# A two-block network on one core: sums of the second layer in PSUM banks, squares gathered by VectorE, modulation tiles loaded as their places become free

## The reference, cut to what matters

```python
shift, scale, gate = split(silu(c) @ w_mod[l] + b_mod[l], 3)            # modulation, also for ctx
hx = rmsnorm(x, norm_g[l]) * (1 + scale) + shift                        # hc from ctx likewise
q, k, v, g_att, u_pool, g_pool, a_conv, b_conv, g_conv = split(hx @ w_in[l])
y_att  = rmsnorm(diff_attention(q, k, v), subln_g) * silu(g_att)
y_pool = (window_means(u_pool) - u_pool) @ w_pool * silu(g_pool)        # windows of 2, 4, 8, 16
u      = a_conv * sigmoid(b_conv)
y_conv = silu(layernorm(conv31(u))) @ w_pw2 * silu(g_conv)              # 31 taps, one filter per channel
x = x + gate * (concat(y_att, y_pool, y_conv) @ w_out[l])               # layer 0 updates ctx as well
```

## Time and profile before

| what | value |
|---|---|
| median of three runs | 3333.49 us |
| the profiled execution's own time | 3337.83 us |
| its span (first to last instruction) | 3336.1 us |
| mean granted TensorE clock | 0.972 of full |
| PE busy | 3139.7 us, 94% of the span |
| POOL busy | 1888.6 us, 57% |
| ACT, DVE busy | 1443.5 us, 1289.0 us |
| loads | 609 MB, 183 GB/s over the span |

### The profile page before, as it was taken

One profiled execution on the slowest core, in us unless ns is written; L12 is line 12 of the kernel. 1 busy time (PEld: TensorE's weight loads), 2 busy tenths in 40 slices (PEclk: granted clock), 3 DMA queues, 4 the chain that ended last, 5 costly groups with the idle time before them and its releaser, 6 DMA issues.

```text
span 3336.1 us, 64404 instructions
## 1 busy us (share of the span) xinstructions
PE 3139.7 (94%) x25962; PEld 2818.9 (84%) x25962; DVE 1289.0 (39%) x2057; ACT 1443.5 (43%) x2177; POOL 1888.6 (57%) x756
## 2 busy tenths in 40 slices
PE   6899999999899996999798999899989999999999
PEld 4688887777677995878787888799989999999999
DVE  2138502555101418047305787585423343332000
ACT  3212222566322431247534676565444555554333
POOL 1234543333233558445453655576866888887887
PEclk9999999999899997999898999999999999999999
DMA  9787222211443881223584676444543555554555
GB/s 367 310 334 308 88 101 75 78 68 59 186 168 126 327 328 51 101 101 115 204 350 158 249 271 236 179 152 141 187 151 140 189 177 188 179 185 164 190 189 188
DMA packets 85970, 613.35 MB, mean 184 GB/s; under 512 B 9536, under 2 KB 10816, under 8 KB 12736
## 3 DMA queue, kind: packets, MB, share of 16 engines
q1 hardware_dynamic: 84672, 606.02, 49.3%
q10 hardware_dynamic: 1152, 5.24, 0.4%
HBM read 609.13 MB, written 2.10 MB: 183 GB/s over the span
## 4 chain that ended last, share of the span: by engine, by line
issue 58%; POOL 41%; POOLq 1%; PE 0%; DVE 0%; DVEq 0%
POOL w_low L549 41%; POOLq L544 0%; POOLq L548 0%; POOLq L549 0%; PE bank L585 0%; PE bank L587 0%; PE bank L586 0%; DVE region L2343 0%; DVEq L2343 0%; POOLq L2354 0%
## 5 line engine op out<-in xcount | busy, mean ns | idle before, releaser
L549 POOL TENSOR_TENSOR w_low<-raw,w_high 128x1024 fp32r<-128x1024 f32 x752 | 1888.4, 2525 | 1441.1 <-ACT w_high L1108 1438.3
L585 PE MATMUL bank<-h_high,w_high 128*128 128x256 f32 (+1 forms) x4416 | 1412.5, 320 | 48.5 <-POOL w_low L549 47.1
L586 PE MATMUL bank<-h_low,w_high 128*128 128x256 f32 (+1 forms) x4416 | 1390.6, 315 | 0.0
L587 PE MATMUL bank<-h_high,w_low 128*128 128x256 f32 (+1 forms) x4416 | 1390.5, 315 | 0.0
L1108 ACT ACTIVATE w_high<-raw 128x1024 fp32r<-128x1024 f32 x752 | 786.5, 1054 | 1140.0 <-PE bank L587 670.2
L585 PEld LDWEIGHTS bank<-h_high,w_high 128*128 128x128 f32 x4416 | 846.5, 192 | 136.6 <-issue 44.2
L587 PEld LDWEIGHTS bank<-h_high,w_low 128*128 128x128 f32 x4416 | 845.9, 192 | 51.1
L586 PEld LDWEIGHTS bank<-h_low,w_high 128*128 128x128 f32 x4416 | 846.5, 192 | 49.9 <-issue 0.7
L1108 ACT ACTIVATE region<-bank 128x512 f32<-128x512 f32 (+3 forms) x353 | 163.8, 472 | 390.8 <-PE bank L587 308.5
L563 PE MATMUL bank<-region,vec_sb 128*32 128x128 f32 x6016 | 197.3, 283 | 40.5 <-DMA region<-in_w_mods 40.5
L563 PEld LDWEIGHTS bank<-region,vec_sb 128*32 128x32 f32 x6016 | 164.5, 113 | 74.4 <-DMA region<-in_w_mods 46.0
(11 more groups left out here) (227 smaller groups left out, 3390.7 us busy)
## 6 DMA issues: line engine op xcount, KB each, us to landing
region<-in_w_mods SPq DMA_DIRECT2D x188, 1024.0 KB, 8.0
raw<-in_w_in SPq DMA_DIRECT2D x172, 1024.0 KB, 4.9
raw<-in_w_up SPq DMA_DIRECT2D x88, 1024.0 KB, 4.8
raw<-in_w_out SPq DMA_DIRECT2D x48, 1024.0 KB, 5.4
raw<-in_w_down SPq DMA_DIRECT2D x48, 1024.0 KB, 4.9
raw<-in_w_abr SPq DMA_DIRECT2D x8, 1024.0 KB, 4.9
raw<-in_w_sbr SPq DMA_DIRECT2D x8, 1024.0 KB, 4.8
region<-in_xin SPq DMA_DIRECT2D x1, 4096.0 KB, 14.3
```

Source lines behind the costliest of these rows:

```text
L549: nc.gpsimd.tensor_tensor(WL[s][:, part], RAW[s][:, part], WH[s][:, part], ALU.subtract) \
L585: nc.tensor.matmul(bank[:, 0:n], WH[slot][:, w], h, start=first and j == 0, stop=False)
L586: nc.tensor.matmul(bank[:, 0:n], WH[slot][:, w], l, start=False, stop=False)
L587: end = nc.tensor.matmul(bank[:, 0:n], WL[slot][:, w], h, start=False, stop=last and j == len(blocks) - 1)
```

## The change

1. **Sums in banks.** In layer 1, `small` accumulates the convolution in banks `AUX[0]` and `AUX[3]` and the pooling sums in `AUX[1]` and `AUX[2]`, not in SBUF. Two copies bring the convolution back to SBUF; the final subtraction of the pooling part reads the banks and is four instructions, not one. Layer 0 stays as it is.
2. **Squares on DVE.** ACT squares as before. DVE adds each square to `AUX[0]` (`add_square`), one after the residual of the next tile; the last sum goes to `NT_` in SBUF, and one matmul with ones sums it over the partitions.
3. **Modulation tiles.** In layer 1's input product SP no longer waits for `n_hl`. After `two(1)` it waits until the output product of layer 0 has left the banks, loads the first four modulation tiles, and goes on with `two(2)`. In its output product SP issues `two(1)` (units 2 and 3) first, then two modulation tiles when four heads are gated and two more when all eight are. For that the places of `BUF_OUT1` are in another order.
4. **Distance in the queue.** The weight units keep their place relative to the turn: of the first turn, the loads that were issued already are left out.

```diff
-    BUF_OUT1 = r2(0, 2048, 4096, 6144)
+    BUF_OUT1 = r2(0, 4096, 2048, 6144)
...
-            def with_mods(turns, unit0, per, buffers, i0=0):
+            def with_mods(turns, unit0, per, buffers, after=0, asked=0, loaded=0):
                 slots = len(buffers)
-                with sp.Fori(0, turns) as i:
+                if asked:
+                    for t in range(4):
+                        for q in range(max(per * t, asked), per * (t + 1)):
+                            sp.wait_ge(sem("mod_mm"), unit0 + q - slots + 1)
+                            mod_load(buffers[q % slots], q % slots, unit0 + q)
+                        if t >= loaded:
+                            unit(0, t + 2 + after)
+                with sp.Fori(1 if asked else 0, turns) as i:
...
-                        unit(i, t + 2 + 4 * i0)
+                        unit(i, t + 2 + after)
...
                 if l == 1:
                     two(0)
                     two(1)
-                sp.wait_ge(sem("n_hl"), H_AT[f"in{l}"] + KT)
+                    evacuated(sp, T_OUT[0] + 16)
+                    for q in range(4):
+                        mod_load(BUF_IN1[q], q, M_IN1 + q)
+                else:
+                    sp.wait_ge(sem("n_hl"), H_AT["in0"] + KT)
                 two(2)
...
-                    with_mods(4, M_IN1, 2, BUF_IN1, 1)
+                    with_mods(4, M_IN1, 2, BUF_IN1, 4, 4)
...
-                sp.wait_ge(sem(f"at{l}_y"), 8)
                 if l == 0:
+                    sp.wait_ge(sem("at0_y"), 8)
                     with_mods(3, M_OUT0, 1, BUF_OUT0)
                 else:
-                    with_mods(3, M_OUT1, 2, BUF_OUT1)
+                    two(1)
+                    for q in range(4):
+                        sp.wait_ge(sem("at1_y"), 4 + 4 * (q // 2))
+                        mod_load(BUF_OUT1[q], q, M_OUT1 + q)
+                    with_mods(3, M_OUT1, 2, BUF_OUT1, 0, 4, 2)
...
-                        if end == 4 or s >= 2:
-                            add_squares(name, width, 4 * i + (s - 2), s % 2, end == 1 and s == 2, False)
-            for k in (14, 15):
-                add_squares(name, width, k, k % 2, False, k == 15)
+            pe.wait_ge(sem("n_sums"), N_AT[name])
+            nc.tensor.matmul(AUX[0][:, 0:width], ONES, NT_[:, 3, 0:width], start=True, stop=True) \
+                .then_inc(sem("n_squsd"), 1)
...
+        def add_square(name, n, i, s):
+            count = 16 * N_AT[name] + s + 1 + 4 * i
+            static = isinstance(i, int)
+            dve.wait_ge(sem("n_sq"), count)
+            sq, sums = NT_[:, s % 2, 0:n], AUX[0][:, 0:n]
+            if static and i == 0 and s == 0:
+                V.tensor_copy(sums, sq).then_inc(sem("n_squsd"), 1)
+                return
+            dve.wait_ge(sem("n_squsd"), count + 1)
+            if static and i == 3 and s == 3:
+                add(NT_[:, 3, 0:n], sums, sq).then_inc(sem("n_sums"), 1)
+            else:
+                add(sums, sums, sq).then_inc(sem("n_squsd"), 1)
...
+            in_banks = lambda n0, n1: [AUX[n][:, a:a + T] for n in (n0, n1) for a in (0, T)]
+            conv = in_banks(0, 3) if l else [y[:, 4 + c, :] for c in range(4)]
+            pools = in_banks(1, 2) if l else [y[:, g, :] for g in range(4)]
...
-                    acc = st(y[:, 4 + c, :])[:, :, a:b]
+                    acc = st(conv[c])[:, :, a:b]
...
+            if l:
+                for n in range(2):
+                    own.mark(V.tensor_copy(y[:, 4 + 2 * n:6 + 2 * n, :], AUX[3 * n][:, 0:T2].rearrange("p (c t) -> p c t", t=T)))
+                own.wait()
...
-                    acc = st(y[:, g, :])[:, :, a:b]
+                    acc = st(pools[g])[:, :, a:b]
...
-            sub(y[:, 0:4, :], y[:, 0:4, :], up).then_inc(sem("cv_pool"), 1)
+            for g in range(4):
+                last = sub(y[:, g, :], pools[g], up[:, g, :])
+            last.then_inc(sem("cv_pool"), 1)
...
+                square_before(("in1", "fin")[l], T2, i, s)
...
+            add_square(("in1", "fin")[l], T2, 3, 3)
```

More of the change, by code:

```diff
@@ L473, in stream @@
                     two(1)
-                sp.wait_ge(sem("n_hl"), H_AT[f"in{l}"] + KT)
+                    evacuated(sp, T_OUT[0] + 16)
[3 more added lines that the diff above has]
+                    sp.wait_ge(sem("n_hl"), H_AT["in0"] + KT)
                 two(2)
                 if l == 0:
-                    with_mods(3, M_IN0, 4, BUF_IN0, 1)
+                    with_mods(3, M_IN0, 4, BUF_IN0, 4)
                     start = 9
                 else:
-                    with_mods(4, M_IN1, 2, BUF_IN1, 1)
+                    with_mods(4, M_IN1, 2, BUF_IN1, 4, 4)
                     start = 11
@@ L1717, in norm, with square_before @@
                     low(at_, j, [(lo(j), T_BANK["in1"][j % 4][:, lower], unit + j, col, hi(j))])
+        def add_square(name, n, i, s):
[11 more added lines that the diff above has]
+                add(sums, sums, sq).then_inc(sem("n_squsd"), 1)
+        def square_before(name, n, i, s):
+            if s:
+                add_square(name, n, i, s - 1)
+            elif not (isinstance(i, int) and i == 0):
+                add_square(name, n, i - 1, 3)
         def rope(l, h):
@@ L1741, in small @@
             wdw, bdw = VEC["w_dw"][0] + l * 124, VEC["b_dw"][0] + 4 * l
+            in_banks = lambda n0, n1: [AUX[n][:, a:a + T] for n in (n0, n1) for a in (0, T)]
+            conv = in_banks(0, 3) if l else [y[:, 4 + c, :] for c in range(4)]
+            pools = in_banks(1, 2) if l else [y[:, g, :] for g in range(4)]
             for c in range(4):
-                own.mark(V.tensor_scalar(y[:, 4 + c, :], uc[:, c, :], VE[:, wdw + 31 * c + 15:wdw + 31 * c + 16],
+                own.mark(V.tensor_scalar(conv[c], uc[:, c, :], VE[:, wdw + 31 * c + 15:wdw + 31 * c + 16],
                                          VE[:, bdw + c:bdw + c + 1], ALU.mult, ALU.add))
@@ L1761, in small @@
             for g in range(4):
-                own.mark(V.tensor_copy(y[:, g, :], up[:, g, :]))
+                own.mark(V.tensor_copy(pools[g], up[:, g, :]))
             for off in [o_ for h in range(8) for o_ in (-1 - h, h + 1)][:15]:
@@ L1773, in small @@
                 for s in range(S):
-                    own.mark(mul(st(y[:, g, :])[:, s, :], st(y[:, g, :])[:, s, :], rc[:, g, :]))
+                    own.mark(mul(st(pools[g])[:, s, :], st(pools[g])[:, s, :], rc[:, g, :]))
             own.wait()
-            sub(y[:, 0:4, :], y[:, 0:4, :], up).then_inc(sem("cv_pool"), 1)
+            for g in range(4):
+                last = sub(y[:, g, :], pools[g], up[:, g, :])
+            last.then_inc(sem("cv_pool"), 1)
             dve.wait_ge(sem("cv_sum"), l + 1)
@@ L2308, in _, with residual2 @@
         dve.wait_ge(sem("x_norm"), KT)
-        with dve.Fori(0, 4) as i:
+        def residual2(i, s):
+            n = 4 * i + s
+            dve.wait_ge(halves_done, 2 * U_OUT2 + 2 * n + 2)
+            V.scalar_tensor_tensor(tile(RES, n), L[s][:, 0:T], MODF[:, ds(3 * n + 3 * 128 + 2, 1)], tile(RES, n),
+                                   ALU.mult, ALU.add).then_inc(bank_free[s], 1)
+            square_before("b2", T, i, s)
+        for s in range(4):
+            residual2(0, s)
+        with dve.Fori(1, 4) as i:
             for s in range(4):
[L2311 to L2314, removed]
+                residual2(i, s)
+        add_square("b2", T, 3, 3)
         evacuated(dve, T_OUT2 + 16)
```

## The result

Four runs of the changed kernel gave a median of 3256.43 us (3254.95 to 3260.75), four runs of the kernel before beside them 3330.47 us (3326.89 to 3334.86). The ratio is 0.9779, with an interval of 0.9761 to 0.9797. The forecast was 3254 us, in a range of 3243 to 3278. The profiled execution took 3255.04 us, its span is 3253.3 us.

The account below looks back on a forecast made before the run. PE, busy for 94% of the span, was taken to bound the kernel. 34.4 + 29.0 + 6.0 + 10.5 = 79.9 us off the median of 3333.49 gave 3253.6, said as 3254 us, range 3243 to 3278.

Parts of the forecast that it names:

- Part 1: Layer 1's convolution: with sums in banks POOL no longer stalls beside DVE, nor PE behind it; 34.4 us, bounds 31.7 to 37.
- The rival in which the write or the pointer operand holds POOL: Layer 1's convolution: not the second SBUF input locks POOL out, so banks change nothing; 3288 us, chance 0.08 (stall stays in part).
- The slower rival: Layer 1's sums in banks: a slow write and read-back makes DVE late for PE; above 3333 us, chance 0.03.
- Part 2: Output products of layer 0, layer 1 and second block: squares leave PE, 29.9 less 0.9 for tails, 29.0 us, bounds 26 to 31.
- so 0.6 more: Tail of layer 1's output product: one DVE addition, one matmul and semaphores take 1.8 us after a wait of 1.22 before.
- the 13 x 0.94 us of `in1`: Layer 0's output product: 13 squares ahead of the last product leave PE, 0.94 us each, 12.2 us.
- 13 x 0.42: Second block's output product: 13 squares of 256 columns leave PE, 0.42 us each, 5.5 us.
- Part 3: Layer 1's input and output products: first modulation tiles loaded earlier; 6.0 us (bounds 4.1 to 9.9) and 10.5 us (7 to 13).
- the 0.5 us that the prediction allowed: Layer 1's input product: the tiles behind the early four land at 1121, PE wants them at 1120, some 0.5 us late.
- The clock near 1.00: Sign for part 3: at the head of both layer 1 products, waits of 4.07 and 5.37 us gone, clock near 1.00.
- That the loads bind: Rival in layer 1's output product: saved squares become waits for tiles, early pairs only move waits; 3268 to 3282 us, chance 0.17.
- The estimate of 8.8 us for a tile: Layer 1's output product by the skill's 358 GB/s: squares there give 0.35 us each, not 0.94; sum 72 us.

Follow-up runs that it names:

- the undone part: The changed kernel with one part of the change taken back: without part 1 3293.46 us, without part 2 3280.52 us, without part 3 3271.3 us.
- the pair with the exchanged operands: The changed kernel, layer 1's convolution not accumulated: both tensor inputs in SBUF and output in a bank, 3295.84 us; one input in a bank and output in SBUF, 3259.37 us.

## Why the prediction was right, and where its sizes were off

**Part 1** was right in mechanism and size. The forecast of 34.4 us came from the tiles leaving the banks; the undone part gives 34.4 by the trace. The reading of the earlier trace rows, that one input in a bank leaves POOL free, was the right one, and the pair with the exchanged operands has shown it. The rival in which the write or the pointer operand holds POOL is false.

**The slower rival** is false too. The 120 instructions of the sums in banks take 46.09 us, against 46.60 in SBUF: a chain in a bank costs nothing more than one in SBUF. The rival needed 0.4 us more for each.

**Part 2** was mis-sized: 29.0 us forecast, 24.1 by the undone part. DVE's residuals show where. From the third tile's to the last's `in1` takes 171.7 us before and 161.8 after, `fin` 118.5 and 106.8; from the first's to the last's `b2` takes 91.8 and 86.5. That is 9.9 + 11.7 + 5.3 = 26.9 us for the squares ahead of the last product, where 29.9 was forecast, and the tails cost 2.6 and not 0.9. Both terms are off.

The first is "so 0.6 more ... in `in1` and `b2` ... 0.3 and 0" for the tails. They cost 9.84 - 8.29 = 1.55 us in `in1` and 10.63 - 9.88 = 0.75 in `fin`, 0 to 0.3 in `b2`. The prediction counted one addition of DVE at 0.69 and a matmul at 1.02. ACT does its last two squares one behind the other, so two additions stand in a row behind them. And the matmul of `in1` takes 2.01, behind 2.50 us in which PE has nothing to do. The squares that it used to sum there kept its clock up: with them on PE no trace shows a slow matmul in a tail, without them nine of fourteen do. So the 0.75 of `fin` is a lucky case; in three other traces it is 1.7.

The second is the 13 x 0.94 us of `in1`, which came to 9.9 us and not 12.2. Every fourth tile the square covered a wait that it had hidden: `mod_unit` has to wait until DVE has read the four sums. The timeline of PE at such a tile:

```profile
905.71 0.95 PE L587 MATMUL bank<-const_sb,region 128*128 128x4 f32 x8
907.00 1.08 PE L579 MATMUL bank<-region,vec_sb 128*32 128x128 f32 x32 [0.34 <-DVE mod_sb L1849]
```

From the sums to the next tile it takes 1.29 us now. Before it took 1.84 with the square in between, so the square's leaving gives 0.55 there, not 0.94. The other tiles are 12.13 us apart (DVE's residual begins at 919.23, 931.37 and 943.50) against 12.98 before. That fits the 12.1 that was forecast, but it is 0.85 for a tile: without the square, the step from the last product to the next tile is 0.31 us (918.81 to 919.12), where the one to the square was 0.23. In `fin` and in `b2` the sizes nearly hold: a pair of tiles takes 16.46 us (DVE's residuals at 1610.17 and 1626.63) in place of 18.27, 0.91 for a tile, and in `b2` 5.76 us for a tile as forecast. The row of `b2` in the table has only 3.9 where 13 x 0.42 is 5.5, because the time ahead of its first tile moves by itself: from the split of its first unit to DVE's first residual it is 20.9 us before and 21.9 after, and between 20.1 and 21.9 over the twelve traces. From the first residual to the last, the nine kernels in which DVE gathers squares take 86.3 or 86.5 us, the three others 91.8 to 92.0.

**Part 3** was right within its bounds: 16.5 forecast, 14.9 by the undone part. SP's queue shows that the tiles are asked for early, at 1059.35 instead of behind the norm, and PE goes from unit 3 into the tiles without a wait (the stretch from 1078 to 1106 ran at a clock of 1.00, against 0.79 from 1100 to 1116 before):

```profile
1058.84 0.33 SPq L451 DMA_DIRECT2D raw<-in_w_in  x1
1059.35 2.00 SPq L420 DMA_DIRECT2D region<-in_w_mods  x4
```

```profile
1078.00:1106.00 28.00, 27.61 (x323) 26.74 (x323) 14.81 (x20) 15.66 (x23) 23.45 (x10) 1.00 0.59 217
```

The next pair is late by the 0.5 us that the prediction allowed, or a little more: PE waits 0.73 us for it at 1116.54, and the stretch of units 8 to 20 is 1.0 us longer. Net 7.3 - 1.0 = 6.3, forecast 6.0. In the output product PE now has four tiles in a row and two short waits for the next two, in place of the waits of 5.37 and 3.06 us:

```profile
1582.93 3.70 PE L579 MATMUL bank<-region,vec_sb 128*32 128x128 f32 x128
1587.34 1.05 PE L587 MATMUL bank<-const_sb,region 128*128 128x4 f32 x8 [0.72 <-ACT region L1123]
1589.99 1.08 PE L579 MATMUL bank<-region,vec_sb 128*32 128x128 f32 x32 [1.59 <-DMA region<-in_w_mods]
1593.07 1.94 PE L579 MATMUL bank<-region,vec_sb 128*32 128x128 f32 x32 [2.00 <-DMA region<-in_w_mods]
1594.94 0.58 PE L601 MATMUL bank<-h_high,w_high 128*128 128x256 f32 x1
```

From the first tile to unit 2 it is 12.0 us, where it was 21.5 (1638.65 to 1660.16), so 9.5 are gained against 10.7 forecast. The rest of the term that is missing, 8.2 by the stretch, went to the clock. "The clock near 1.00" failed here: PE still has gaps of 1.59 and 2.00 us, and unit 2 begins at half the clock, with matmuls of 256 columns 0.21 us apart instead of 0.12.

```profile
1582.00:1604.00 22.00, 17.69 (x321) 16.26 (x319) 2.13 (x5) 6.98 (x10) 9.94 (x5) 0.84 0.96 390
```

**That the loads bind** did not come true. Over 118 us of the output product the queue is as full as it was in the input product, and carries 382 GB/s:

```profile
1582.00:1700.00 118.00, 113.69 (x1642) 109.20 (x1641) 16.87 (x34) 42.79 (x61) 64.98 (x28) 0.97 0.96 382
```

After the two waits at its head PE waits for no tile there, and the tiles are 8.23 us apart, as close as PE can take them. The estimate of 8.8 us for a tile, with the 358 GB/s of the Trainium skill (SBUF — State Buffer, "Summary: rules for kernel authors"), doesn't fit this trace, and it didn't fit the 380 and 422 GB/s of the earlier trace rows either. PE's whole wait for modulation tiles fell from 40.5 to 32.0 us. The margin is small, though: with the DMA engines at 96%, little more could be taken from PE's work there before it turned into waits. That is argued, not tried.

The forecast of 3254 us was 2.4 us under the median. 79.9 us were expected and 74.0 came between the medians; the 6 us between are the squares and their tails, some 5 us, and the slow clock at the head of the output product. That the number still came out so close is luck in part: with a fourth run of the kernel before, of 3326.89 us, its median fell from the 3333.49 that the forecast started from to 3330.47. From there the forecast would have been 3250.6, 5.8 us off. Beside the later experiments the kernel before had medians of 3332.34, 3333.83 and 3331.95 us.

## What to carry to other kernels

When two engines hold each other up, look at the operands of each instruction, not at how busy either is: one tensor input moved into a bank freed POOL for 44 us, and with it PE for 34, while DVE did the same work in the same time. When work is taken off the busiest engine, ask of each piece what wait it was covering: ahead of `mod_unit` a square of 0.94 us was worth only 0.55, and behind the last product the squares cost PE nothing and kept its clock up, so those are best left where they were. And a wait that is moved along a queue is worth only as much as the engine at its end, here DVE, gets done in the meantime.

## What the runs showed that was not expected

One POOL instruction that takes 2.39 us by itself took 46.68 while 120 instructions of DVE ran back to back, 0.39 us apart. It got in between no two of them in any of the three traces with both of DVE's tensor inputs in SBUF (before, part 1 undone, output alone in a bank). It does not always take that long: in the kernel with only the pooling sums in SBUF, one POOL instruction, of 5.47 us, waited through some nine of DVE's additions, which start 0.33 us apart and last 0.41, so that each begins before the last has ended. It was done 2.2 us behind the first addition that began after such an end (1289.59, against 1289.56). The convolution's instructions overlap like this all through (0.45 to 0.47 us long). Whether POOL gets its turn only where that overlap stops is a guess; no run was made to test it.

The other way round it holds too. In the kernel with ACT's tables one unit later, from 1743 to 1751, small DVE instructions with inputs in SBUF alone waited for one POOL instruction each:

```profile
1743.24 2.45 DVE L1681 TENSOR_TENSOR second_space<-second_space 128x64 f32<-128x64 f32 x1
1745.72 2.28 DVE L2097 TENSOR_SCALAR second_space<-second_space 128x64 f32<-128x64 f32 x1
1748.04 2.35 DVE L1681 TENSOR_TENSOR second_space<-second_space 128x64 f32<-128x64 f32 x1
1750.42 0.20 DVE L2097 TENSOR_SCALAR second_space<-second_space 128x64 f32<-128x64 f32 x1
```

```profile
1743.20 7.11 POOL L565 TENSOR_TENSOR w_low<-raw,w_high 128x1024 fp32r<-128x1024 f32 x3 [3.36 <-ACT w_high L1123]
```

Three of POOL's instructions ran in a row, and three of DVE's of 64 columns took 2.28 to 2.45 us, against 0.20 to 0.23 when POOL was idle. The one with a single tensor input (L2097) is among them. That one SBUF tensor input leaves the two free of each other is shown for the convolution's `scalar_tensor_tensor` only; with `tensor_scalar` DVE waited for POOL. So the chain that ACT's `trig()` waits for is long in part because POOL splits weights beside it. Whether its gain could be had by another order there was not tried.
